# Windowed attention stage: the probabilities' copy is split over ScalarE and VectorE, the inverse is widened on VectorE, and transposes go ahead of scores

## The chip, the cores and the metric

The kernel runs as one program on one core of a Trainium2 chip. It uses the core's engines side by side: TensorE (PE for its matmuls, PEld for its weight loads), VectorE (DVE), ScalarE (ACT), GpSimd (POOL) and SyncE (SP), which here only issues DMAs. Each engine works through its own list of instructions in order; engines wait for one another by semaphores. The metric is the device time of one execution in microseconds.

## The reference

The program is one deep block (windowed attention beside a bidirectional mLSTM, an expert feed-forward) followed by two more layers. The change touches only the windowed attention, which is this part of the reference (8 query heads of 64 columns, 1024 tokens, 256 context tokens, blocks of 128 queries that see the 128 keys before and after them):

```python
def latent_attention(q, k, v, k_ctx, v_ctx, sink):
    ...
    def one_block(args):
        qb, kb, vb, n = args
        ...
        s_loc = jnp.einsum('bqkgd,bskd->bkgqs', qb, kb, preferred_element_type=f32) * scale
        s_loc = jnp.where(ok, s_loc, NEG)
        s_ctx = jnp.einsum('bqkgd,bckd->bkgqc', qb, k_ctx, preferred_element_type=f32) * scale
        s_sink = jnp.broadcast_to(sink_f[None, :, :, None, None], s_loc.shape[:-1] + (1,))
        p = jax.nn.softmax(jnp.concatenate([s_loc, s_ctx, s_sink], -1), -1)
        p_loc = p[..., :span].astype(vb.dtype)
        p_ctx = p[..., span:span + L].astype(vb.dtype)
        return (jnp.einsum('bkgqs,bskd->bqkgd', p_loc, vb)
                + jnp.einsum('bkgqc,bckd->bqkgd', p_ctx, v_ctx))

    o = lax.map(one_block, (q_blk, k_blk, v_blk, jnp.arange(nb)))
```

## The kernel before

The attention stage is `phase_attention`. Its work is cut into 64 units `u`: a unit is one head and one block of 128 queries. Units 2i and 2i+1 are a pair `i` (two heads `a` = 0 and 1, the same block `n`), and there are 32 pairs, 8 blocks for each of 4 values of `j`. A unit has the keys of the context (2 tiles of 128) and of its neighbourhood (3 tiles; 2 in the first and last block). So of 16 units 12 have five tiles and 4 have four; the text calls them long and short.

The order of the work is written out by hand, one list for each engine, with a loop over `u`:

- TensorE: `score(u+2)` makes the scores of two units ahead (4 matmuls into `ps[:, a]`, from `q_st` and the high and low parts of the keys). `turn(u)` transposes the probabilities `p` tile by tile into the PSUM tensor `pt` (called `win_t` in the trace), of which there is one. `weigh(i, ...)` multiplies the turned probabilities by the values, in two pieces: tiles 0 to 2 at even `u`, the rest at odd `u`, for the pair `u // 2 - 1`. Ahead of the first piece it also transposes the pair's inverse denominators, widened to 128 columns, into the second half of `po` (`win_o`).
- VectorE: `largest(u+2)` adds the mask (`win_s`, line 1207; in block 0 the sink too, line 1198) and takes the negative row maximum (line 1209). At odd `u`, `invert(u // 2)` comes before it: the reciprocal of a pair's two denominators (2 columns, line 1216). At even `u`, `take_out(u // 2 - 2)` comes after it: it copies the transposed inverse out of PSUM into `spread` (line 1223) and multiplies the output by it (line 1227).
- ScalarE: `exps(u+1)` makes the probabilities and their sum (line 1169), `take(u)` copies the whole turned unit from `pt` to `p_t` (line 1177, 640 or 512 columns).
- GpSimd: `widen(i)` spreads the two inverses over 128 columns (line 1063). Between two widenings it also does `split_q(j)`, the split of the next two heads' queries into a high and a low part (lines 1076 and 1082), and `pre.split`, the split of two weight tiles for the next stage (lines 336 and 339). It does `split_q(1)` ahead of all widenings, `pre.split` after pair 2, and `split_q(2)` and `split_q(3)` after pairs 8 and 16.

The waits that matter below: `score(u)` waits for `exps(u-2)`, since both use the same half of `ps`; `turn(u)` waits for `exps(u)` and for the copy of unit u-1 out of `pt`; the first piece of `weigh(i)` waits for `widen(i)`.

Of the kernel before, what the change touches and what calls it, by code (L numbers as in the profile page):

```python
# [16 lines left out]
ALU = mybir.AluOpType  # L17
# [3 lines left out]
P = 128  # L21
# [10 lines left out]
N_HEADS, HEAD_DIM = 8, 64  # L32
# [151 lines left out]
def build_program(nc, A, out):  # L184
    with ExitStack() as ctx:
# [786 lines left out]
        def phase_attention():  # L972
# [19 lines left out]
            den = mem("att_den", [P, 2, 2])  # L992
            inverse = mem("att_inverse", [P, 2, 2])
            wide = mem("att_inverse_wide", [P, 2, P])
            spread = mem("att_spread", [P, P])
            zeros = mem("att_zeros", [P, P])
# [11 lines left out]
            probs = sem("win_probs")  # L1008
            p_turned = sem("win_p_turned")
            p_t_out = sem("win_p_t_out")  # L1010
            widened = sem("win_widened")
            inverse_done = sem("win_inverse_done")
# [15 lines left out]
            with nc.psum_tensor("win_s", [P, 2, 2, HALF], F32) as ps, nc.psum_tensor("win_t", [P, 2, HALF], F32) as pt, \  # L1028
# [28 lines left out]
                @block.gpsimd  # L1057
                def _(pool):
                    def widen(i):
                        pool.wait_ge(inverse_done, i + 1)  # L1060
                        if i >= 2:
                            pool.wait_ge(weighed, i - 1)
# [3 lines left out]
                    def split_q(j):  # L1066
                        if j >= 2:
                            pool.wait_ge(scores, 2 * BLOCKS * (j - 1))
                            pool.wait_ge(stacked[j], 32)
                            pool.wait_ge(pre.lo_done, 2)  # L1070
                        for a in range(2):
                            if a:
                                pool.wait_ge(hi_done, 2 * (j - 1) + a)
                            elif j >= 2:
                                pool.wait_ge(widened, BLOCKS * (j - 1) + 1)
# [8 lines left out]
                    pool.memset(zeros[:], 0.0).then_inc(zeroed, 1)  # L1084
                    pool.wait_ge(zeroed, 1)
                    pool.wait_ge(stacked[0], 32)
                    pool.wait_ge(stacked[1], 32)
                    split_q(1)
                    pool.wait_ge(lo_done, 2)
                    for i in range(PAIRS):  # L1090
                        widen(i)
                        if i == 2:
                            pool.wait_ge(widened, i + 1)
                            pre.split(pool)
                        if i % BLOCKS == 0 and BLOCKS <= i < PAIRS - BLOCKS:
                            split_q(i // BLOCKS + 1)
                            pool.wait_ge(lo_done, 2 * (i // BLOCKS + 1))

                @block.tensor
                def _(pe):  # L1100
# [18 lines left out]
                    def turn(u):  # L1119
                        j, n, a = unit(u)  # L1120
                        pe.wait_ge(probs, u + 1)
                        if u:
                            pe.wait_ge(p_t_out, u)
                        for t in range(len(tiles(n))):
                            ins = pe.transpose(pt[:, t // 4, t % 4 * P:(t % 4 + 1) * P], p[u % NP][:, 1 + t * P:1 + (t + 1) * P], ident)
                        ins.then_inc(p_turned, 1)

                    def weigh(i, begin, end):
                        n = i % BLOCKS
                        values = tiles(n)  # L1130
                        if begin == 0:
                            pe.wait_ge(widened, i + 1)
                            if i >= 2:
                                pe.wait_ge(o_out, i - 1)
                            pe.transpose(po[:, i % 2, P:2 * P], wide[:, i % 2, :], ident)
                            pe.wait_ge(p_t_out, 2 * i + 2)
                        for t in range(begin, min(end, len(values))):
# [18 lines left out]
                def _(act):  # L1156
# [4 lines left out]
                    def exps(u):  # L1161
# [3 lines left out]
                        if u >= NP:  # L1165
                            act.wait_ge(p_turned, u - NP + 1)
                        if u >= 4:
# [3 lines left out]

                    def take(u):
                        nt = len(tiles(unit(u)[1]))
                        act.wait_ge(p_turned, u + 1)
                        if u >= NT:
                            act.wait_ge(weighed, u // 2 - 1)
                        act.copy(p_t[:, u % NT, 0:nt, :], pt[:].rearrange("p b (t q) -> p (b t) q", q=P)[:, 0:nt, :]).then_inc(p_t_out, 1)

                    exps(0)
                    for u in range(U):  # L1180
                        if u + 1 < U:
                            exps(u + 1)
                        take(u)

                @block.vector
                def _(dve):
# [6 lines left out]
                    def largest(u):  # L1193
# [11 lines left out]
                        else:  # L1205
# [4 lines left out]
                                          ALU.max, negate=True).then_inc(max_done, 1)  # L1210

                    def invert(i):
                        dve.wait_ge(probs, 2 * i + 2)
                        if i >= 2:
                            dve.wait_ge(widened, i - 1)
                        dve.reciprocal(inverse[:, i % 2, :], den[:, i % 2, :]).then_inc(inverse_done, 1)

                    def take_out(i):
                        j, n = i // BLOCKS, i % BLOCKS
                        dve.wait_ge(weighed, i + 1)  # L1220
                        if i:
                            dve.wait_ge(o_out, i)
                        dve.tensor_copy(spread[:], po[:, i % 2, P:2 * P]).then_inc(spread_out, 1)
# [3 lines left out]
                        dve.tensor_tensor(out_now[:, j % 2, n * P:(n + 1) * P], po[:, i % 2, 0:P], spread[:], ALU.mult).then_inc(o_out, 1)  # L1227
# [2110 lines left out]
```

## Time and profile before

| | us |
|---|---|
| median of 3 runs | 3813.88 |
| lowest and highest run | 3810.36, 3817.38 |
| the profiled execution's own time | 3813.88 |
| its span | 3811.9 |
| attention stage: first score matmul to the last output product | 214.8 to 369.2 |
| loop of the units: first transpose (219.3) to the last product | 149.9 |

The profile gives every group of instructions a line: the source line, the engine, the operation, the tensors written and read, how many there were, the busy time and the mean duration, and then how long the engine had been idle just before them and who ended that idle time. A timeline row gives the start in us, the duration in us and the number of instructions merged. Starts are counted from the beginning of the span. The end of a matmul is modelled, so for TensorE the distances between starts say more than durations do.

### The profile page before, as it was taken

The page shows a single profiled execution, that of the slowest core. Times are in us where ns is not written, and L with a number is a line of the kernel's source. Part 1 is how long each engine was busy: PE and PEld are TensorE (multiplying, and loading weights), DVE is VectorE, ACT ScalarE, POOL GpSimd, SP SyncE. Part 2 cuts the span into 40 slices and gives each one's busy share as a digit, 9 for nine tenths or more (in the row PEclk, how much of TensorE's full clock was granted, in tenths as well). Part 3 has the DMA queues.
Part 4 walks back from the last instruction along what each step waited for, and adds up shares of the span by engine and source line. Part 5 has one row for each costly group of instructions (what it writes and reads, how often), then busy time and mean ns, then how long its engine had stood idle before and what let it go on. Part 6 is the DMA issues. An engine that isn't in the chain of part 4 may idle for free. (4 is left out here: it accounts for less than half of the span.)

```text
span 3811.9 us, 45383 instructions
## 1 busy us (share of the span) xinstructions
PE 3474.8 (91%) x16720; PEld 2808.0 (74%) x16720; DVE 1414.2 (37%) x1976; ACT 1100.2 (29%) x1654; POOL 1380.6 (36%) x678
## 2 busy tenths in 40 slices
PE   8978997779588868999999899999999999999988
PEld 3757885656466646777787688888888888888877
DVE  5566223653666655331111333221222222222232
ACT  4145223431455522100110211111323232232332
POOL 2331331432455545333333444443332333333222
PEclk9979997889799878999999899999999999999999
DMA  8221111043688862132112211132211221121122
GB/s 296 47 78 34 39 28 59 0 137 130 231 300 293 296 178 84 50 110 65 44 39 93 72 50 50 50 110 72 40 39 39 39 45 39 39 39 39 39 56 83
DMA packets 417567, 340.21 MB, mean 89 GB/s; under 512 B 83526, under 2 KB 355706, under 8 KB 417346
## 3 DMA queue, kind: packets, MB, share of 16 engines
q1 hardware_dynamic: 333916, 296.54, 24.7%
q10 hardware_dynamic: 78950, 25.62, 3.1%
q0 software_dynamic: 4608, 16.78, 1.9%
q8 instruction: 62, 1.02, 0.1%
q14 instruction: 31, 0.25, 0.0%
HBM read 287.06 MB, written 48.43 MB: 88 GB/s over the span
## 5 line engine op out<-in xcount | busy, mean ns | idle before, releaser
L273 POOL TENSOR_TENSOR w_hi<-w_raw,zero_col 128x1024 fp32r<-128x1024 f32 x193 | 366.1, 1897 | 1589.4 <-PE first_z L308 640.3
L276 POOL TENSOR_TENSOR w_lo<-w_raw,w_hi 128x1024 fp32r<-128x1024 f32 x193 | 499.5, 2588 | 15.2
L308 PE MATMUL first_z<-h_hi,w_hi 128*128 128x512 f32 x1216 | 392.7, 404 | 4.4 <-DVE h_lo L2059 4.4
L308 PE MATMUL first_z<-h_lo,w_hi 128*128 128x512 f32 x1216 | 377.2, 391 | 0.0
L308 PE MATMUL first_z<-h_hi,w_lo 128*128 128x512 f32 x1216 | 375.6, 390 | 0.0
L308 PEld LDWEIGHTS first_z<-h_hi,w_lo 128*128 128x128 f32 x1216 | 228.8, 188 | 49.7
L308 PEld LDWEIGHTS first_z<-h_lo,w_hi 128*128 128x128 f32 x1216 | 228.9, 188 | 48.8
L308 PEld LDWEIGHTS first_z<-h_hi,w_hi 128*128 128x128 f32 x1216 | 220.3, 189 | 43.4 <-DVE h_lo L2059 4.6
L308 PE MATMUL dil_z<-h_hi,w_hi 128*128 128x512 f32 x640 | 219.0, 423 | 0.6 <-POOLq L264 0.6
L308 PE MATMUL dil_z<-h_lo,w_hi 128*128 128x512 f32 x640 | 199.6, 393 | 0.0
L3251 DVE SCALAR_TENSOR_TENSOR dil_biased<-const,dil_slope_now,dil_aux 128x128 f32<-128x128 f32 (+1 forms) x192 | 78.5, 409 | 322.7 <-PE dil_aux L3103 312.1
L308 PE MATMUL dil_z<-h_hi,w_lo 128*128 128x512 f32 x640 | 197.4, 390 | 0.0
L2387 POOL TENSOR_TENSOR lo_down<-raw_down,hi_down 128x4096 fp32r<-128x4096 f32 x15 | 135.0, 9000 | 149.2 <-ACT hi_down L2475 149.2
L2516 DVE TENSOR_TENSOR lo_gate<-raw_gate,hi_gate 128x2048 fp32r<-128x2048 f32 x30 | 127.1, 4238 | 92.7 <-ACT hi_gate L2475 92.7
L3193 ACT ACTIVATE dil_p<-dil_biased,dil_neg_max 128x128 f32<-128x128 f32 (+1 forms) x192 | 86.3, 450 | 219.8 <-DVE dil_neg_max L3255 219.7
L3294 DVE COPY dil_p_t<-dil_aux 128x128 f32<-128x128 f32 (+1 forms) x192 | 67.8, 353 | 204.2 <-PE dil_aux L3118 181.9
L308 PEld LDWEIGHTS dil_z<-h_hi,w_lo 128*128 128x128 f32 x640 | 120.1, 188 | 27.8
L308 PEld LDWEIGHTS dil_z<-h_lo,w_hi 128*128 128x128 f32 x640 | 120.0, 188 | 26.0
L308 PEld LDWEIGHTS dil_z<-h_hi,w_hi 128*128 128x128 f32 x640 | 112.7, 189 | 16.2 <-POOLq L264 1.0
L3186 ACT ACTIVATE dil_k<-first_z 128x1024 f32<-128x1024 f32 x24 | 40.3, 1680 | 215.4 <-PE first_z L308 121.8
L308 PE MATMUL mls_z<-h_hi,w_hi 128*128 128x512 f32 (+1 forms) x344 | 94.4, 373 | 6.3 <-DVEq L1363 5.9
L336 POOL TENSOR_TENSOR w_hi<-w_raw,zero_col 128x1024 fp32r<-128x1024 f32 x22 | 42.6, 1935 | 153.4 <-DMA w_raw<-in_w_in 62.8
(563 smaller groups left out, 7218.4 us busy)
## 6 DMA issues: line engine op xcount, KB each, us to landing
w_raw<-in_odd_w_in SPq DMA_DIRECT2D x112, 512.0 KB, 3.7
raw_gate<-in_w_gate SPq DMA_DIRECT2D x16, 2048.0 KB, 8.3
raw_up<-in_w_up SPq DMA_DIRECT2D x16, 2048.0 KB, 10.0
raw_down<-in_w_down SPq DMA_DIRECT2D x16, 2048.0 KB, 7.5
w_raw<-in_even_w_in SPq DMA_DIRECT2D x40, 512.0 KB, 3.8
start_w_mod<-in_w_mod SPq DMA_DIRECT2D x16, 1024.0 KB, 7.9
w_raw<-in_w_in SPq DMA_DIRECT2D x16, 512.0 KB, 3.7
w_raw<-in_even_w_out SPq DMA_DIRECT2D x16, 512.0 KB, 3.9
```

The lines of the kernel that those rows point to most:

```text
L273: pool.tensor_tensor(w_hi[:, u], w_raw[:, u], zero_col[:, 0:1].to_broadcast([P, KT * P]).rearrange("p (k n) -> p k n", k=KT), ALU.add).the ...
L276: pool.tensor_tensor(w_lo[:, u], w_raw[:, u], w_hi[:, u].bitcast(F32), ALU.subtract).then_inc(self.split, 1)
L308: ins = pe.matmul(z, w[:, u, kt], rhs[:, kt, c0:c0 + width], start=first, stop=last)
L336: pool.tensor_tensor(w_hi[:, u], w_raw[:, u], zero_col[:, 0:1].to_broadcast([P, KT * P]).rearrange("p (k n) -> p k n", k=KT), ALU.add).the ...
L2387: pool.tensor_tensor(w_lo_["down", slot][:], raw["down", slot][:], w_hi_["down"][:].bitcast(F32), ALU.subtract).then_inc(split["down"], 1)
L2516: dve.tensor_tensor(w_lo_["gate", slot][:, kts], raw["gate", slot][:, kts], w_hi_["gate"][:, kts].bitcast(F32), ALU.subtract).then_inc(spl ...
L3186: act.activation(to, in_banks(z[t % 2][:], t // 2 if t < VT else t - VT), ACT.Copy, scale=P ** -0.5 if t < VT and t % 2 else 1.0).then_inc ...
L3193: act.activation(probs[u][:], biased[:, u % 2, 0:w], ACT.Exp, bias=neg_max[:, u:u + 1], accum_out=den[:, u:u + 1]).then_inc(exp_done, 1)
L3251: dve.scalar_tensor_tensor(out=biased[:, u % 2, 0:w], in0=dist, scalar=slope_now[:, g, :], in1=aux[:, uses % 2, 0:w], op0=ALU.mult, op1=AL ...
L3294: dve.tensor_copy(p_t[:, u % 2, 0:w], aux[:, uses % 2, 0:w]).then_inc(aux_free[uses % 2], 1)
```

## The change

It edits four of the engines' lists in `phase_attention` and nothing else.

- VectorE's reciprocal now reads each of the two denominators 64 times over (a broadcast view) and writes 128 columns; `wide` and `widen` are gone, and with them GpSimd's part in every pair. GpSimd does its three `split_q` and `pre.split` in a plain loop.
- `turn(u)` puts tiles 0 to 2 into the first bank of `pt` and the rest into the second (before: four and one), and signals twice. The copy out of `pt` is split: ScalarE's `take_near` takes 384 columns, VectorE's new `take_far` takes 256 (128 in a short unit). `turn(u)` waits for both copies of unit u-1.
- TensorE does `turn(u)` ahead of `score(u+2)`, where it did it behind.
- VectorE does `take_far(u)` behind `largest(u+2)`.
- The copy of the transposed inverse to `spread` moves from VectorE to ScalarE (`take_spread`, at odd `u`), and `spread` gets two buffers.

```diff
@@ block.gpsimd
-                    def widen(i):
-                        pool.wait_ge(inverse_done, i + 1)
-                        ...
-                        pool.tensor_tensor(wide[:, i % 2, :].rearrange("p (a d) -> p a d", a=2), inverse[:, i % 2, :].unsqueeze(2).to_broadcast([P, 2, HEAD_DIM]),
-                                           zero_col[:, 0:1].unsqueeze(2).to_broadcast([P, 2, HEAD_DIM]), ALU.add).then_inc(widened, 1)
@@ block.tensor
                         pe.wait_ge(probs, u + 1)
                         if u:
-                            pe.wait_ge(p_t_out, u)
+                            pe.wait_ge(near_out, u)
+                            pe.wait_ge(far_out, u)
                         for t in range(len(tiles(n))):
-                            ins = pe.transpose(pt[:, t // 4, t % 4 * P:(t % 4 + 1) * P], p[u % NP][:, 1 + t * P:1 + (t + 1) * P], ident)
-                        ins.then_inc(p_turned, 1)
+                            to = pt[:, 0, t * P:(t + 1) * P] if t < 3 else pt[:, 1, (t - 3) * P:(t - 2) * P]
+                            ins = pe.transpose(to, p[u % NP][:, 1 + t * P:1 + (t + 1) * P], ident)
+                            if t == 2:
+                                ins.then_inc(near_turned, 1)
+                        ins.then_inc(far_turned, 1)
 ...
                         if begin == 0:
-                            pe.wait_ge(widened, i + 1)
+                            pe.wait_ge(inverse_done, i + 1)
 ...
                     for u in range(U):
+                        turn(u)
                         if u + 2 < U:
                             score(u + 2)
-                        turn(u)
                         if u >= 2:
                             weigh(u // 2 - 1, *((0, 3) if u % 2 == 0 else (3, 5)))
@@ block.scalar
-                        act.copy(p_t[:, u % NT, 0:nt, :], pt[:].rearrange("p b (t q) -> p (b t) q", q=P)[:, 0:nt, :]).then_inc(p_t_out, 1)
+                        act.copy(p_t[:, u % NT, 0:3, :], pt[:, 0, 0:3 * P].rearrange("p (t q) -> p t q", q=P)).then_inc(near_out, 1)
+
+                    def take_spread(i):
+                        act.wait_ge(weighed, i + 1)
+                        if i >= 2:
+                            act.wait_ge(o_out, i - 1)
+                        act.copy(spread[:, i % 2, :], po[:, i % 2, P:2 * P]).then_inc(spread_out, 1)
@@ block.vector
+                    def take_far(u):
+                        j, n, a = unit(u)
+                        nt = len(tiles(n)) - 3
+                        dve.wait_ge(far_turned, u + 1)
+                        if u >= NT:
+                            dve.wait_ge(weighed, u // 2 - 1)
+                        dve.tensor_copy(p_t[:, u % NT, 3:3 + nt, :], pt[:, 1, 0:nt * P].rearrange("p (t q) -> p t q", q=P)).then_inc(far_out, 1)
+
 ...
-                        dve.reciprocal(inverse[:, i % 2, :], den[:, i % 2, :]).then_inc(inverse_done, 1)
+                        dve.reciprocal(inverse[:, i % 2, :].rearrange("p (a d) -> p a d", a=2), den[:, i % 2, :].unsqueeze(2).to_broadcast([P, 2, HEAD_DIM])).then_inc(inverse_done, 1)
 ...
                         if u + 2 < U:
                             largest(u + 2)
+                        take_far(u)
                         if u >= 4 and u % 2 == 0:
                             take_out(u // 2 - 2)
```

TensorE's list, before, in the middle of the loop, from one unit's transposes to the next unit's. `win_s` are score matmuls, `win_t` transposes of probabilities, `win_o` the inverse's transpose and the weighing.

```order
L1125 MATMUL win_t<-const,att_p_1473 128x128 x5
L1135 MATMUL win_o<-const,att_inverse_wide 128x128
L1139 MATMUL win_o<-att_p_t,v_rows 64x128 x6
L1115 MATMUL win_s<-k_hi,q_st 128x256
L1116 MATMUL win_s<-k_hi,q_st 128x384
L1115 MATMUL win_s<-k_lo,q_st 128x256
L1116 MATMUL win_s<-k_lo,q_st 128x384
L1125 MATMUL win_t<-const,att_p_1474 128x128 x5
L1139 MATMUL win_o<-att_p_t,v_rows 64x128 x4
```

The same place after the change, from the transposes of one unit to those of the next.

```order
L1112 MATMUL win_t<-const,att_p_1474 128x128 x5
L1100 MATMUL win_s<-k_hi,q_st 128x256
L1101 MATMUL win_s<-k_hi,q_st 128x384
L1100 MATMUL win_s<-k_lo,q_st 128x256
L1101 MATMUL win_s<-k_lo,q_st 128x384
L1130 MATMUL win_o<-att_p_t,v_rows 64x128 x4
L1112 MATMUL win_t<-const,att_p_1472 128x128 x5
```

The transposes stood behind the scores of the unit two ahead and now stand in front of them; the weighing is last in both.

VectorE's list, before, over one pair: mask and maximum at an even unit, the output, then the inverse, mask and maximum at the odd unit.

```order
L1207 TENSOR_TENSOR win_s<-win_s,const 128x2x128
L1209 TENSOR_REDUCE att_neg_max<-win_s 128x1
L1223 COPY att_spread<-win_o 128x128
L1227 TENSOR_TENSOR att_out_now<-win_o,att_spread 128x128
L1216 RECIPROCAL att_inverse<-att_den 128x2
L1207 TENSOR_TENSOR win_s<-win_s,const 128x2x128
L1209 TENSOR_REDUCE att_neg_max<-win_s 128x1
```

The same pair on VectorE after the change.

```order
L1206 TENSOR_TENSOR win_s<-win_s,const 128x2x128
L1208 TENSOR_REDUCE att_neg_max<-win_s 128x1
L1217 COPY att_p_t<-win_t 128x256
L1230 TENSOR_TENSOR att_out_now<-win_o,att_spread 128x128
L1223 RECIPROCAL att_inverse<-att_den 128x128
L1206 TENSOR_TENSOR win_s<-win_s,const 128x2x128
L1208 TENSOR_REDUCE att_neg_max<-win_s 128x1
L1217 COPY att_p_t<-win_t 128x256
```

In each unit a copy of `win_t` has come behind the maximum of the unit two ahead; the copy to `att_spread` is gone, and the reciprocal writes 128 columns instead of 2.

## Rows read from the trace of the kernel before

**Rows 1.** The page's head: span and instructions.
```profile
span 3811.9 us, 45383 instructions
```

**Rows 2.** Window of one pair: PE, PEld, DVE, ACT, POOL busy; granted clock; DMA.
```profile
284.70:288.90 4.20, 4.20 (x42) 3.44 (x39) 3.11 (x8) 3.18 (x7) 0.40 (x1) 1.00 0.00 0
```

**Rows 3.** Waits in 216 to 369 us: total us, times, longest.
```profile
DVE win_s L1207 <- PE win_s L1116: 48.5, 56, 6.1
...
PE win_o L1135 <- POOL att_inverse_wide L1063: 13.2, 4, 3.7
```

**Rows 4.** Timeline of that pair: start, us, engine, line, operation.
```profile
284.74 0.39 PE L1115 MATMUL win_s<-k_hi,q_st 128*128 128x256 f32 x1
...
285.63 0.43 DVE L1207 TENSOR_TENSOR win_s<-win_s,const 128x256 f32<-128x256 f32 x1 [0.36 <-PE win_s L1116]
...
286.10 0.82 DVE L1209 TENSOR_REDUCE att_neg_max<-win_s 128x1 f32<-128x641 f32 x1
...
287.36 0.71 PE L1125 MATMUL win_t<-const,att_p 128*128 128x128 f32 x5
...
287.90 0.27 PE L1135 MATMUL win_o<-const,att_inverse_wide 128*128 128x128 f32 x1
...
288.91 0.39 PE L1115 MATMUL win_s<-k_hi,q_st 128*128 128x256 f32 x1
```

**Rows 5.** Timeline: scores, mask and maximum of a short unit.
```profile
292.96 0.39 PE L1115 MATMUL win_s<-k_hi,q_st 128*128 128x256 f32 x1
...
293.73 0.30 DVE L1207 TENSOR_TENSOR win_s<-win_s,const 128x128 f32<-128x128 f32 x1 [0.51 <-PE win_s L1116]
294.06 0.69 DVE L1209 TENSOR_REDUCE att_neg_max<-win_s 128x1 f32<-128x513 f32 x1
```

**Rows 6.** VectorE groups of the span: PSUM copies, reciprocals (busy us, mean ns | idle).
```profile
L3294 DVE COPY dil_p_t<-dil_aux 128x256 f32<-128x256 f32 x88 | 37.4, 425 | 52.5 <-PE dil_aux L3118 38.7 <-DVE dil_p_t L3294 12.7
...
L3294 DVE COPY dil_p_t<-dil_aux 128x128 f32<-128x128 f32 x104 | 30.4, 292 | 151.7 <-PE dil_aux L3118 143.2 <-DVE dil_p_t L3294 8.3
...
L940 DVE RECIPROCAL qk_rstd<-qk_rstd 128x1024 f32<-128x1024 f32 x4 | 26.2, 6553 | 0.7 <-DVE k_cm L957 0.2
...
L3269 DVE RECIPROCAL dil_den<-dil_den 128x24 f32<-128x24 f32 x8 | 2.4, 296 | 0.0
```

**Rows 7.** Timeline at the loop's start.
```profile
218.10 0.55 PE L1115 MATMUL win_s<-k_hi,q_st 128*128 128x256 f32 x1 [1.23 <-ACT att_p L1169]
...
219.30 1.06 PE L1125 MATMUL win_t<-const,att_p 128*128 128x128 f32 x4
```

**Rows 8.** Timeline at the loop's end.
```profile
363.68 0.69 ACT L1177 COPY att_p_t<-win_t 128x640 f32<-128x640 f32 x1 [0.76 <-PE win_t L1125]
...
364.51 0.63 PE L1125 MATMUL win_t<-const,att_p 128*128 128x128 f32 x4 [0.29 <-ACT att_p_t L1177]
...
368.89 0.29 DVE L1227 TENSOR_TENSOR att_out_now<-win_o,att_spread 128x128 f32<-128x128 f32 x1
```

**Rows 9.** Windows of TensorE behind a stall: busy, granted clock, DMA.
```profile
273.00:276.00 3.00, 3.00 (x17) 0.50 0.69 175
...
279.00:282.00 3.00, 3.00 (x31) 1.00 0.02 5
```

**Rows 10.** Timeline of a long unit at the low clock.
```profile
229.40 0.58 PE L1115 MATMUL win_s<-k_hi,q_st 128*128 128x256 f32 x1
...
230.64 1.27 PE L1125 MATMUL win_t<-const,att_p 128*128 128x128 f32 x5
230.88 0.43 DVE L1207 TENSOR_TENSOR win_s<-win_s,const 128x256 f32<-128x256 f32 x1 [6.13 <-PE win_s L1116]
```

**Rows 11.** Windows of TensorE in the mLSTM stage.
```profile
746.00:750.00 4.00, 3.64 (x30) 1.00 0.00 0
750.00:754.00 4.00, 2.41 (x20) 1.00 0.00 0
...
758.00:762.00 4.00, 1.55 (x8) 0.71 0.00 0
```

More of the change, by code:

```diff
@@ L992, in phase_attention @@
             den = mem("att_den", [P, 2, 2])
-            inverse = mem("att_inverse", [P, 2, 2])
-            wide = mem("att_inverse_wide", [P, 2, P])
-            spread = mem("att_spread", [P, P])
+            inverse = mem("att_inverse", [P, 2, P])
+            spread = mem("att_spread", [P, 2, P])
             zeros = mem("att_zeros", [P, P])
@@ L1008, in phase_attention @@
             probs = sem("win_probs")
-            p_turned = sem("win_p_turned")
-            p_t_out = sem("win_p_t_out")
-            widened = sem("win_widened")
+            near_turned = sem("win_near_turned")
+            far_turned = sem("win_far_turned")
+            near_out = sem("win_near_out")
+            far_out = sem("win_far_out")
             inverse_done = sem("win_inverse_done")
@@ L1058, in _ @@
                 def _(pool):
-                    def widen(i):
-                        pool.wait_ge(inverse_done, i + 1)
-                        if i >= 2:
-                            pool.wait_ge(weighed, i - 1)
-                        pool.tensor_tensor(wide[:, i % 2, :].rearrange("p (a d) -> p a d", a=2), inverse[:, i % 2, :].unsqueeze(2).to_broadcast([P, 2, HEAD_DIM]),
-                                           zero_col[:, 0:1].unsqueeze(2).to_broadcast([P, 2, HEAD_DIM]), ALU.add).then_inc(widened, 1)
-                    def split_q(j):
+                    pool.memset(zeros[:], 0.0).then_inc(zeroed, 1)
+                    pool.wait_ge(zeroed, 1)
+                    pool.wait_ge(stacked[0], 32)
+                    pool.wait_ge(stacked[1], 32)
+                    for j in range(1, N_HEADS // 2):
                         if j >= 2:
@@ L1082, in split_q @@
                             pool.tensor_tensor(q_lo[own[a], :], q_cm[own[a], j, :], q_st[own[a], j % 2, a, :].bitcast(F32), ALU.subtract).then_inc(lo_done, 1)
[L1084 to L1093, printed above, removed]
+                        if j == 1:
+                            pool.wait_ge(lo_done, 2 * j)
                             pre.split(pool)
-                        if i % BLOCKS == 0 and BLOCKS <= i < PAIRS - BLOCKS:
-                            split_q(i // BLOCKS + 1)
-                            pool.wait_ge(lo_done, 2 * (i // BLOCKS + 1))
                 @block.tensor
@@ L1131, in weigh @@
                         if begin == 0:
-                            pe.wait_ge(widened, i + 1)
+                            pe.wait_ge(inverse_done, i + 1)
                             if i >= 2:
                                 pe.wait_ge(o_out, i - 1)
-                            pe.transpose(po[:, i % 2, P:2 * P], wide[:, i % 2, :], ident)
-                            pe.wait_ge(p_t_out, 2 * i + 2)
+                            pe.transpose(po[:, i % 2, P:2 * P], inverse[:, i % 2, :], ident)
+                            pe.wait_ge(near_out, 2 * i + 2)
+                        else:
+                            pe.wait_ge(far_out, 2 * i + 2)
                         for t in range(begin, min(end, len(values))):
@@ L1182, in _ @@
                             exps(u + 1)
-                        take(u)
+                        take_near(u)
+                        if u >= 3 and u % 2:
+                            take_spread(u // 2 - 1)
+                    take_spread(PAIRS - 1)
                 @block.vector
@@ L1214, in invert @@
                         if i >= 2:
-                            dve.wait_ge(widened, i - 1)
-                        dve.reciprocal(inverse[:, i % 2, :], den[:, i % 2, :]).then_inc(inverse_done, 1)
+                            dve.wait_ge(weighed, i - 1)
+                        dve.reciprocal(inverse[:, i % 2, :].rearrange("p (a d) -> p a d", a=2), den[:, i % 2, :].unsqueeze(2).to_broadcast([P, 2, HEAD_DIM])).then_inc(inverse_done, 1)
                     def take_out(i):
                         j, n = i // BLOCKS, i % BLOCKS
[L1220 to L1223, printed above, removed]
                         dve.wait_ge(spread_out, i + 1)
```

11 lines of the change are left out of this document (5 added, 6 removed).

## The prediction

> **What bounds the kernel now.** The span [rows 1] is a chain of stages; the edit lies in one of them, 214.8 to 369.2 us, so I read only that stage. First its windows: over a pair of long units TensorE is busy 4.20 of 4.20 us, VectorE 3.11 and ScalarE 3.18, at the full clock (granted 1.00) [rows 2]. Second the waits: TensorE waits for a widened inverse 4 times, 13.2 us in all, and VectorE waits for scores nearly every unit, 48.5 us in all [rows 3]. Third the timeline: the scores of two neighbouring pairs start 4.17 us apart (284.74 and 288.91) [rows 4]. So the loop goes at TensorE's pace, 2.09 us a unit, and the other two engines wait for it. The exceptions are the four waits: GpSimd's widening stands behind a split of queries or weights on its own queue. Behind such a wait TensorE also runs at the lower of its two levels, 1.2 GHz: granted 0.50 in 273 to 276 us, full again (2.4 GHz) in 279 to 282 [rows 9].
>
> From the first transpose, 219.30, to the transposes of unit 62, 364.51 [rows 7, 8], there are 62 steps in 145.2 us: 2.34 us a unit with the stalls in it, against 2.09 without.
>
> **The change, part by part.**
>
> *Widening on VectorE.* The four waits for GpSimd go, 13.2 us, and the low-clock stretches behind them. If TensorE stayed the bound, the loop would fall to about 62 x 2.09 = 129.6 us (short units are a little quicker): 16 us saved. The price is a reciprocal over 128 columns. From 24 columns in 296 ns and 1024 in 6553 ns [rows 6] one more column costs (6553 - 296) / 1000 = 6.3 ns, so 128 cost 0.296 + 104 x 0.0063 = 0.95 us, once a pair. It is a broadcast read, which the rows do not show; bounds are the 0.30 us of 24 columns and twice the 0.95.
>
> *The copy to `spread`* (about as long as the 128-column copy, 292 ns) goes from VectorE to ScalarE. ScalarE gives up 256 of 640 columns of copy in return, so it stays well under its 3.18 us a pair. It costs nothing while a unit takes over 1.59 us, the half of 3.18.
>
> *The split copy and the order.* This is where it is decided. `turn(u+1)` waits for `take_far(u)`. On VectorE `take_far(u)` stands behind `largest(u+2)`, which waits for `score(u+2)`. On TensorE `score(u+2)` now stands behind `turn(u)`. So there is one closed ring per unit: transposes of u, scores of u+2, mask and maximum of u+2, copy of u, transposes of u+1. Before, `take(u)` on ScalarE needed only `turn(u)` and `exps(u+1)`, not the scores of u+2, and VectorE was not in any one-unit ring; scores of u+2 and VectorE's work on them covered one another's units. Now TensorE can do beside VectorE's part only the weighing. The ring of a long unit:
>
> - transposes to scores: 5 transposes take 287.90 - 287.36 = 0.54 us up to the next matmul [rows 4], 0.56 with the longer weight load of a score;
> - start of the scores to the mask: 285.63 - 284.74 = 0.89 [rows 4];
> - mask to the end of the maximum: 286.10 + 0.82 - 285.63 = 1.29 [rows 4];
> - the copy of 256 columns from PSUM: 0.425 [rows 6], with 0.04 to start: 0.47;
> - its semaphore to the next transpose: ScalarE's copy ended at 364.37 and the waiting transpose started at 364.51 [rows 8]: 0.14. From VectorE it is not shown; bounds 0.04 and 0.24.
>
> Sum 3.35 us. A short unit: 0.45 + (293.73 - 292.96 = 0.77) + (294.06 + 0.69 - 293.73 = 1.02) + 0.33 (292 ns copy) + 0.14 = 2.71 [rows 5, 6]. With 12 long and 4 short in 16: 3.19; with 0.01 for the sink column, 3.20.
>
> *What hides beside the ring.* After the copy of an even unit VectorE also does the output product (about 0.3) and the reciprocal (0.95), 1.3 us with the gaps. It has 0.14 + 0.56 + 0.89 = 1.59 us until the next scores come. So the reciprocal is hidden by 0.3 us; at twice its length it would add 0.65 us a pair, 20 us. The weighing (0.6 to 0.8 us) lies beside mask and maximum (1.29). ScalarE's exponentials of u+1 start when the maximum of u+1 is known and end before the transposes that want them. GpSimd's splits now start as early as their inputs allow and nobody waits for them.
>
> *The clock.* In a long unit TensorE works about 2.0 of 3.35 us and is then idle for 1.3. In the mLSTM stage it was busy 3.64 and 2.41 of 4 us in two windows in a row at a granted 1.00, and fell to 0.71 in one with 1.55 of 4 [rows 11]. The loop, at 60%, is like the 2.41 of 4, so I take the full clock. The start is at the low clock before [rows 10], and three units of it stay there. A low unit costs more: the five transposes 1.27 - 0.71 = 0.56 and the scores up to the mask (230.88 - 229.40 = 1.48) - 0.89 = 0.59 [rows 4, 10], together 1.15. Three times 1.15 is 3.4 us.
>
> *The sum.* `turn(0)` moves from behind the scores of unit 2 to in front: from 219.30 to about 218.24 (these scores started at 218.10, on the same release). Unit 62 is turned at 218.2 + 62 x 3.20 + 3.4 = 420.0 us. The tail stays as it was, 368.89 + 0.29 - 364.51 = 4.7 us [rows 8]: it has no ring, but one wide reciprocal in it and a copy on another engine. End of the stage 424.7 against 369.2: 55.5 us longer. The profiled execution's own time is 3813.88, the same as the median, with a span of 3811.9. So 3813.9 + 55.5 = 3869.
>
> **The rivals.**
>
> *TensorE stays the bound (faster).* If the ring took under 2.34 us a unit (146.3 us over 62 steps is 2.36 with the earlier start), the removed waits would win: 3814 - 16 = 3798. For it speaks that VectorE's sum of work is small, about 4.6 us a pair with the new copies and reciprocal, which over 32 pairs is 147 us, just what the loop takes today. Against it: that is a sum over work that could overlap, and here it stands in one ring with TensorE; mask, maximum and scores alone are 2.18 us, so the transposes and the copy would have to cost 0.2 where rows give about 1.2.
>
> *The clock falls for the whole loop.* Then each long unit takes 4.50 us, and it is 3869 + 59 x 1.15 = 3937. A third of the units low gives 3892. For it: there is idle time in every unit, which the loop of before did not have. Against it: [rows 11], and that at the low clock a unit would keep TensorE busy about 3.9 of 4.5 us, under which the clock came back in [rows 9]. The Trainium skill, page "TensorE: Matmul & The Clock Gate", section "A second HAM failure mode: psum-queue depth-cycling", says that a TensorE that idles briefly between groups of matmuls while it cycles through PSUM banks can swing between its half and full clock. By that rule about half the units would be low, 3903; the mLSTM windows here do not bear it out.
>
> *VectorE's list is the bound inside the slower loop.* If the broadcast reciprocal took twice its width's price, 3869 + 20 = 3889.
>
> *The change does not do what it says.* The four waits could return at another place, since `exps` and `weigh` still wait for `invert`. `invert` of a pair is done at the odd unit, the first piece of its weighing a unit later, so no wait is late; if they did return it would add 13 us, 3882.
>
> **How the numbers follow.** The ring at the full clock: 0.77. The low clock for a third or more of the loop: 0.12. The doubled reciprocal or returned waits: 0.05. TensorE as the bound: 0.04. Something between that loses nothing and wins nothing: 0.02. The predicted time is 3869. Its own range: the semaphore's bounds give 6 us either way, the transposes 4, the copy 4, the start 3 down and 7 up: 3855 to 3886. To leave out no more than 2 in 10 I reach up to the partly low clock: 3854 to 3898. A change of 0.2%, 7.6 us, is about what a measurement of this kernel can tell from none. Faster by more than that 0.04, within it 0.02, slower 0.94.
>
> **What would show it.** The stage should end near 425 us, and neighbouring long units' transposes should start 3.35 us apart at a granted clock near 1.00. The waits should show TensorE's `win_t` waiting for VectorE's `att_p_t` some 60 times, 1.2 to 1.5 us each, and no wait of `win_o` for an inverse; VectorE's wait for scores should be near 0.3 us at odd units and near 1.6 at even ones. The reciprocal should show at 0.95 us and have nobody waiting. The prediction is wrong if `win_t` waits for ScalarE or not at all, or if transposes lie 2.1 us apart.

## The result, and the profile after

The change makes the kernel slower: 3851.41 us (median of 4 runs, 3847.47 to 3854.53) against 3815.63 (4 runs), a ratio of 1.0095 with a 95% interval of 1.0078 to 1.0112. That is 35.8 us more, where 55.5 were forecast; 3851.4 lies 2.6 us under the range's low end of 3854. The direction and the mechanism were right, the size was not. The profiled execution of the changed kernel took 3854.16 us.

From here on the attention stage is measured in one way for all kernels: from the start of the first exponential to the end of the last output product. It was 369.18 - 217.18 = 152.0 us and is 411.25 - 215.70 = 195.6, 43.5 us more. Below are the head of the page after the change, then the rows that mark the stage's first exponential, the transposes of unit 62 and the last output product:

```profile
span 3852.2 us, 45443 instructions
```

```profile
215.70 0.69 ACT L1160 ACTIVATE att_p<-win_s,att_neg_max 128x513 f32<-128x513 f32 x1 [2.49 <-DVE att_neg_max L1208]
```

```profile
406.61 0.63 PE L1112 MATMUL win_t<-const,att_p 128*128 128x128 f32 x4 [0.95 <-DVE att_p_t L1217]
...
410.96 0.29 DVE L1230 TENSOR_TENSOR att_out_now<-win_o,att_spread 128x128 f32<-128x128 f32 x1 [0.99 <-ACT att_spread L1173]
```

The waits of the stage (total us, times, longest), to be set beside [rows 3]:

```profile
PE win_t L1112 <- DVE att_p_t L1217: 61.9, 61, 1.7
DVE win_s L1206 <- PE win_s L1101: 57.4, 56, 2.6
```

There is a new wait, TensorE's transposes for VectorE's copy of `win_t`: 61 times, 61.9 us. The four waits of `win_o` for a widened inverse, 13.2 us, are gone.

The timeline of one long unit at the full clock, to be set beside [rows 4]. It shows the ring in the order of its steps:

```profile
286.79 0.74 PE L1112 MATMUL win_t<-const,att_p 128*128 128x128 f32 x5 [1.22 <-DVE att_p_t L1217]
...
287.29 0.36 PE L1100 MATMUL win_s<-k_hi,q_st 128*128 128x256 f32 x1
...
288.16 0.43 DVE L1206 TENSOR_TENSOR win_s<-win_s,const 128x256 f32<-128x256 f32 x1 [1.51 <-PE win_s L1101]
...
288.62 0.82 DVE L1208 TENSOR_REDUCE att_neg_max<-win_s 128x1 f32<-128x641 f32 x1
289.37 0.41 DVE L1217 COPY att_p_t<-win_t 128x256 f32<-128x256 f32 x1
...
289.70 0.28 DVE L1230 TENSOR_TENSOR att_out_now<-win_o,att_spread 128x128 f32<-128x128 f32 x1
...
289.89 0.94 DVE L1223 RECIPROCAL att_inverse<-att_den 128x128 f32<-128x128 f32 x1
289.93 0.74 PE L1112 MATMUL win_t<-const,att_p 128*128 128x128 f32 x5 [0.89 <-DVE att_p_t L1217]
...
291.29 0.43 DVE L1206 TENSOR_TENSOR win_s<-win_s,const 128x256 f32<-128x256 f32 x1 [0.45 <-PE win_s L1101]
```

The transposes of two neighbouring units start at 286.79 and 289.93, 3.14 us apart, and before every one of them stands a wait for VectorE (0.89 and 1.22 us in turn). The scores start 0.50 us behind the transposes, the mask 0.87 behind the scores. The reciprocal (289.89, 0.94 us) ends at 290.83, and the next mask starts only at 291.29, after a wait of 0.45 us for the scores: it is hidden.

One window of two long units, as [rows 2] was of two (PE, PEld, DVE, ACT, POOL busy; clock; DMA), and one of the loop's middle:

```profile
284.00:290.26 6.26, 4.15 (x41) 3.31 (x40) 4.23 (x9) 2.99 (x9) 0.00 (x0) 1.00 0.00 0
```

```profile
300.00:340.00 40.00, 27.07 (x257) 21.42 (x255) 27.49 (x57) 19.53 (x47) 8.49 (x4) 1.00 0.09 27
```

No engine is full any more: TensorE is busy 27.07 of 40 us, VectorE 27.49 and ScalarE 19.53. This is what a ring looks like in a profile: TensorE and VectorE are each idle a third of the time and each waits for the other.

### The profile page after: what moved, and what is told of

It is laid out like the page before. It is cut to its first block and busy times, and to the rows that moved or that the text cites. A ratio compares the mean times of both kernels' runs of the same rounds, so it can differ in the third digit from the quotient of the medians.

```text
span 3852.2 us, 45443 instructions
## 1 busy us (share of the span) xinstructions
PE 3462.8 (90%) x16720; PEld 2795.9 (73%) x16720; DVE 1445.4 (38%) x2008; ACT 1098.3 (29%) x1686; POOL 1368.9 (36%) x646
## 5 line engine op out<-in xcount | busy, mean ns | idle before, releaser
L273 POOL TENSOR_TENSOR w_hi<-w_raw,zero_col 128x1024 fp32r<-128x1024 f32 x193 | 365.6, 1895 | 1677.0 <-PE first_z L308 640.3
L1112 PE MATMUL win_t<-const,att_p 128*128 128x128 f32 x304 | 47.7, 288 | 63.1 <-DVE att_p_t L1217 61.9
L3190 ACT ACTIVATE dil_k<-first_z 128x1024 f32<-128x1024 f32 x24 | 40.3, 1681 | 218.3 <-PE first_z L308 121.8
```

Source lines behind the costliest of these rows:

```text
L273: pool.tensor_tensor(w_hi[:, u], w_raw[:, u], zero_col[:, 0:1].to_broadcast([P, KT * P]).rearrange("p (k n) -> p k n", k=KT), ALU.add).the ...
L1112: ins = pe.transpose(to, p[u % NP][:, 1 + t * P:1 + (t + 1) * P], ident)
L3190: act.activation(to, in_banks(z[t % 2][:], t // 2 if t < VT else t - VT), ACT.Copy, scale=P ** -0.5 if t < VT and t % 2 else 1.0).then_inc ...
```

## The experiments

All ratios are to the kernel before, run beside them on the same chip. Where a pace is given in us a unit, it is the mean distance between the transposes of unit 44 and those of unit 60, a whole period of 16 units without a stall. It is 2.00 in the kernel before (328.79 to 360.80 us) and 2.98 in the changed one (353.36 to 401.11).

**Cut the ring on VectorE** (`far_first`).

```diff
 (changed kernel, block.vector)
+                        take_far(u)
                         if u + 2 < U:
                             largest(u + 2)
-                        take_far(u)
```

> Theory (a ring per unit through transposes, scores, mask and maximum, and the copy of win_t): with VectorE's copy of win_t ahead of the maximum of the unit two ahead, the copy waits only for the transposes, so the ring is cut. What is left is a ring over two units (exponentials, transposes, scores, mask and maximum: about 3.8 us, 1.9 a unit) and VectorE's own work, 3.8 to 4.6 us a pair. Units 2.1 to 2.3 us apart; TensorE's wait for the copy under 0.2 us; kernel near 3803 us, 45 to 55 below the changed kernel and some 10 below the kernel before. Rival (VectorE has too much work, whatever the order): units stay near 3.1 us apart, kernel near 3850.

Measured: ratio 0.9958 (0.9943 to 0.9972), 3796.8 us, 13.5 under the kernel before and 55 under the changed one, which ran in another session. The stage took 135.5 us (first exponential 216.25, last product 351.75), the pace is 2.05 us a unit, a little quicker than the 2.1 to 2.3 expected, and no wait of TensorE for VectorE's copy is left. The window of the middle of the loop:

```profile
300.00:340.00 40.00, 38.61 (x366) 31.11 (x366) 38.23 (x81) 26.50 (x68) 0.00 (x0) 1.00 0.04 15
```

The same work, in another order, keeps TensorE busy 38.61 of 40 us and VectorE 38.23. So VectorE's work was never too much; its place in the list was. The rival falls.

**Cut the ring on TensorE** (`scores_first`).

```diff
 (changed kernel, block.tensor)
-                        turn(u)
                         if u + 2 < U:
                             score(u + 2)
+                        turn(u)
```

> Theory (the ring): with the scores of u+2 again ahead of the transposes of u, and the copy still behind the maximum, the scores no longer wait for the copy of the unit before, so the ring is cut here too. VectorE waits for scores and then does mask, maximum, copy; units 2.1 to 2.4 us apart, kernel 3800 to 3812. Rival (the split of the copy over two engines is what costs, by its semaphores and VectorE's place in the chain): units stay over 2.8 us apart, kernel over 3835.

Measured: 0.9955 (0.9936 to 0.9973), 3795.2 us, stage 138.1 us (216.20 to 354.25). That is 5 us better than the lower end of what was expected; the pace of 2.11 us a unit is inside it. Here the copy still stands behind the maximum, and nearly all of its cost is gone all the same. It takes both orders together to close the ring; either cut is worth the same within the intervals.

**Take VectorE's copy out of the ring** (`whole_copy`).

```diff
 (changed kernel)
-                            to = pt[:, 0, t * P:(t + 1) * P] if t < 3 else pt[:, 1, (t - 3) * P:(t - 2) * P]
+                            to = pt[:, t // 4, t % 4 * P:(t % 4 + 1) * P]
...
-                        act.copy(p_t[:, u % NT, 0:3, :], ...)
+                        act.copy(p_t[:, u % NT, 0:nt, :], ...)
...
-                        take_far(u)
```

The waits go with the copy: one signal behind the last transpose, one behind ScalarE's copy.

> The turned unit is packed and copied whole by ScalarE again; the wide reciprocal, the move of the spread copy and the transposes ahead of the scores stay. Theory (the ring goes through VectorE's copy alone): no ring per unit, units at TensorE's pace of 2.1 us, no waits for a widened inverse; kernel near 3800, some 15 below the kernel before. Rival (transposes ahead of scores cost by themselves, since scores come 0.5 us later to the maximum and the exponentials): units 2.4 us or more apart, kernel 3820 or more.

Measured: 0.9952 (0.9934 to 0.9970), 3794.5 us, stage 136.6 us, pace 2.09. As the theory said, within the intervals. The split of the copy, which is the change's own idea, brought nothing measurable in this order of TensorE's list: `far_first`, with the ring cut and the copy split, is as fast as this with the copy whole.

**The order on TensorE alone** (`turn_first`): the kernel before, with the two calls swapped as in the change.

> The kernel before with only the two calls on TensorE swapped, transposes of u ahead of scores of u+2. Theory (this order is harmless without VectorE's copy behind the maximum; the ring over two units is 3.8 us, 1.9 a unit, under TensorE's 2.1): within 5 us of the kernel before. Rival (transposes first is itself what costs): 20 us or more slower.

Measured: 1.0011 (1.0001 to 1.0020), 5 us more by the medians (3816.5 against 3811.5), stage 155.2 us against 152.0. Its waits:

```profile
ACT att_p L1169 <- DVE att_neg_max L1209: 48.1, 62, 2.5
...
PE win_t L1125 <- ACT att_p_t L1177: 7.1, 23, 0.9
```

The order is nearly harmless alone, and far from the rival's 20 us. It is not free: the transposes now come 23 times before ScalarE's copy of the unit before has ended, 7.1 us in all, where this happened once, 0.3 us, in the kernel before. The exponentials, which waited for the maximum 8 times (4.5 us) before, now wait 62 times (48.1 us).

**Lengthen the ring** (`ring_plus`). The tensor `neg_max` also gets 32 columns instead of 4, to hold the unused results.

```diff
 (changed kernel, take_far)
+                        dve.tensor_reduce(neg_max[:, 4 + u % 28:5 + u % 28], pt[:, 1, 0:nt * P], AX_X, ALU.max)
                         dve.tensor_copy(p_t[:, u % NT, 3:3 + nt, :], pt[:, 1, 0:nt * P].rearrange("p (t q) -> p t q", q=P)).then_inc(far_out, 1)
```

> The changed kernel with one operation more in the ring: a maximum over the same 256 (or 128) columns of win_t in PSUM on VectorE just ahead of its copy; its result is not used. It takes 0.4 us (0.29 in short units). Theory (everything in the ring costs its whole length each unit): units 0.35 us further apart, 62 x 0.35 = 20 to 25 us more than the changed kernel, near 3875. Rival (the pace is set elsewhere, VectorE waits 57 us for scores anyway): under 5 us more.

Measured: 1.0161 (1.0144 to 1.0178), 3872.1 us against 3850.3 for the changed kernel in the same session, 21.8 more and inside the 20 to 25 expected; stage 214.1 us (216.80 to 430.88), 18.5 more; pace 3.32. The timeline of a long unit with it:

```profile
288.34 0.82 DVE L1208 TENSOR_REDUCE att_neg_max<-win_s 128x1 f32<-128x641 f32 x1
289.08 0.41 DVE L1217 TENSOR_REDUCE att_neg_max<-win_t 128x1 f32<-128x256 f32 x1
...
289.42 0.41 DVE L1218 COPY att_p_t<-win_t 128x256 f32<-128x256 f32 x1
...
289.98 0.97 PE L1112 MATMUL win_t<-const,att_p 128*128 128x128 f32 x5 [0.45 <-DVE att_p_t L1218]
```

The added operation lasts 0.41 us, but from its start to the copy's start there are 0.34 (289.08 to 289.42), and units moved from 3.13 to 3.47 us apart (the last row's transposes are longer because the clock had dipped for a moment there; the 3.47 are from its neighbours). The ring pays for every operation in it, and it pays the distance between starts, not the duration. That distance is the clue to the forecast's error below.

**Shorten what hides beside the ring** (`after_small`).

```diff
 (changed kernel, invert)
-                        dve.reciprocal(inverse[:, i % 2, :].rearrange("p (a d) -> p a d", a=2), den[:, i % 2, :].unsqueeze(2).to_broadcast([P, 2, HEAD_DIM])).then_inc(inverse_done, 1)
+                        dve.reciprocal(small[:, i % 2, :], den[:, i % 2, :]).then_inc(small_done, 1)
+                        dve.wait_ge(small_done, i + 1)
+                        dve.tensor_copy(inverse[:, i % 2, :].rearrange("p (a d) -> p a d", a=2), small[:, i % 2, :].unsqueeze(2).to_broadcast([P, 2, HEAD_DIM])).then_inc(inverse_done, 1)
```

> The changed kernel with a cheaper widening on VectorE: the reciprocal of 2 columns (0.155 us), then a broadcast copy to 128 columns (0.2 us), in place of the 0.94 us reciprocal. Theory (the reciprocal lies hidden in VectorE's wait for scores, 0.45 us of which are left at odd units): no change, within 3 us of the changed kernel. Rival (the reciprocal delays mask and maximum): up to 0.6 us a pair, 15 to 19 us faster.

Measured: 1.0115 (1.0098 to 1.0132), 3854.7 us; the changed kernel in the same session had 1.0101 (1.0084 to 1.0118), 3850.3. No gain: the 4.4 us more lie beyond the 3 that were expected, but the intervals overlap. The stage took 197.9 us (216.97 to 414.83), 2.3 more, at the same pace of 2.99 a unit. Most of that comes from two places, and both lie at a broadcast copy. Here is one, with GpSimd's split of the queries beside it (two operations in one row):

```profile
266.41 4.86 POOL L1081 TENSOR_TENSOR q_lo<-q_cm,q_st 64x1024 fp32r<-64x1024 f32 x2
...
266.66 2.19 DVE L1227 COPY att_inverse<-att_small 128x128 f32<-128x128 f32 x1
...
270.19 0.63 PE L1114 MATMUL win_t<-const,att_p 128*128 128x128 f32 x4 [2.00 <-DVE att_p_t L1219]
```

The broadcast copy, 0.23 us in the median, lasts 2.19 us here and again at 315.55, where GpSimd has just begun the same split (315.29). Each time TensorE's transposes come 3.68 us after the last ones instead of 2.57; behind the second the clock also falls for a moment. The wide reciprocal of the changed kernel took 940 to 946 ns in all 32 cases, beside GpSimd or not.

What the cheaper widening set free turned into waiting, as the mask of an odd unit shows:

```profile
285.34 0.16 DVE L1225 RECIPROCAL att_small<-att_den 128x2 f32<-128x2 f32 x1
...
285.53 0.23 DVE L1227 COPY att_inverse<-att_small 128x128 f32<-128x128 f32 x1
...
286.73 0.43 DVE L1208 TENSOR_TENSOR win_s<-win_s,const 128x256 f32<-128x256 f32 x1 [0.98 <-PE win_s L1103]
```

It waits 0.98 us for the scores where it waited 0.45, and units stay 3.13 us apart.

**The changed kernel again** (`after_again`).

> The changed kernel once more, beside the kernel before on one chip. The two first traces differ by 43.5 us in the attention stage (first exponential to last product) and by 40.3 us in span, the medians by 35.8. Theory (the rest is scatter between runs outside the stage): stage again 195 to 196 us, and more runs bring the difference of the medians to 38 to 44 us. Rival (something outside the stage got quicker with the change): difference again 34 to 37 us, with a stage that is 43 us longer.

Measured: 1.0101 (1.0084 to 1.0118), 3850.3 us against 3811.5, 38.8 us more; stage 195.6 us (216.60 to 412.18). The stage repeats to 0.1 us. The difference of the medians falls between the two bounds that were named: just inside the theory's 38 to 44, and with an interval (32 to 45 us) that holds the rival's 34 to 37 too. This does not settle it.

**The useful part alone** (`wide_only`, and once more as `wide_again`): the kernel before, whose GpSimd list and `invert` are those of the change.

```diff
 (kernel before)
-                            pe.wait_ge(widened, i + 1)
+                            pe.wait_ge(inverse_done, i + 1)
...
-                        dve.reciprocal(inverse[:, i % 2, :], den[:, i % 2, :]).then_inc(inverse_done, 1)
+                        dve.reciprocal(inverse[:, i % 2, :].rearrange("p (a d) -> p a d", a=2), den[:, i % 2, :].unsqueeze(2).to_broadcast([P, 2, HEAD_DIM])).then_inc(inverse_done, 1)
```

> The kernel before with only the reciprocal widened on VectorE and GpSimd's widening gone. Theory (TensorE is the bound, the reciprocal's 0.94 us fits in VectorE's idle time): the four waits, 13.2 us, and the low clock behind them go, 13 to 18 us saved, kernel 3798 to 3802. VectorE's work is 4.0 to 4.1 us a pair against TensorE's 4.17. Rival (VectorE then is too full, the reciprocal in front of the maximum delays the exponentials): units over 2.2 us apart, less than 5 us saved.

> The kernel before with only the wide reciprocal on VectorE, once more, beside its neighbours. Stage 130 to 131.5 us from first exponential to last product, kernel 24 to 28 us under the kernel before.

Measured: 0.9926 (0.9909 to 0.9944), 3784.3 us, and 0.9935 (0.9922 to 0.9949), 3786.6 us. This beats both kernels, by 26 and 27 us against the one before. The stage took 130.8 and 131.0 us, 21 less than 152.0. The window of the loop's middle, of `wide_again`:

```profile
300.00:340.00 40.00, 40.00 (x378) 33.05 (x378) 36.30 (x72) 29.40 (x61) 0.00 (x0) 1.00 0.04 15
```

TensorE is busy 40.00 of 40 us. The saving is more than the 16 us that the forecast had given to the waits, and more than the 13 to 18 expected here. The pace is 2.00 us a unit (in `wide_again` 307.50 to 339.51), as it already was in the kernel before between its stalls; I had taken 2.09 from a single pair of long units and had named the short units as "a little quicker" without counting them. Over 62 units that is 5.6 us, which makes the 21 us of the stage. The 5 or 6 us between these and the medians' 26 and 27 no run explains.

**Three neighbours of it**: the cheap widening (`wide_small`), ScalarE's copy to `spread` (`wide_spread`), and both (`small_spread`), edited as in the experiments above and in the change.

> The kernel before with VectorE widening by a reciprocal of 2 columns and a broadcast copy (0.35 us in place of 0.94 a pair). Theory (the loop is at TensorE's pace already): within 3 us of the wide reciprocal. Rival (VectorE at 4.0 of 4.0 us a pair is the bound there): units 0.05 to 0.15 us closer, 3 to 9 us faster than the wide reciprocal.

> The kernel before with the wide reciprocal and the copy to spread on ScalarE. Theory (ScalarE's copy waits for the weighing in front of the next exponentials, and delays them): equal to or up to 6 us slower than the wide reciprocal alone. Rival (VectorE is the bound and wins 0.28 us a pair): up to 9 us faster.

> The small reciprocal with broadcast copy on VectorE, and the copy to spread on ScalarE. Theory (ScalarE's queue is what the moved copy loads): slower than or equal to the small reciprocal without the move, by 0 to 6 us. Rival: faster than it by 3 us or more.

Measured: 0.9935, 0.9936 and 0.9935, each with the interval 0.9922 to 0.9949 (medians 3790.4, 3788.2 and 3790.7 us, against 3786.6 for `wide_again`); stages of 131.7, 131.4 and 132.8 us. All four are the same within the intervals. With TensorE full, VectorE's 36.30 us of 40 in the wide form against 31.89 in the small one make no difference. The window of `wide_small`:

```profile
300.00:340.00 40.00, 40.00 (x379) 33.00 (x378) 31.89 (x82) 30.27 (x60) 0.00 (x0) 1.00 0.04 15
```

`wide_spread` also shows what the ring's two halves cost once the ring is open. It differs from `whole_copy` in TensorE's order alone, and from `scores_first` in the split of the copy alone. Here is the same window of the three, in the order `wide_spread`, `whole_copy`, `scores_first`:

```profile
300.00:340.00 40.00, 40.00 (x378) 32.92 (x377) 33.83 (x62) 31.22 (x71) 0.00 (x0) 1.00 0.04 15
```

```profile
300.00:340.00 40.00, 38.23 (x361) 30.45 (x361) 32.51 (x60) 29.61 (x69) 0.00 (x0) 1.00 0.04 15
```

```profile
300.00:340.00 40.00, 39.08 (x358) 31.00 (x356) 37.65 (x80) 27.24 (x66) 0.00 (x0) 1.00 0.04 15
```

The paces are 2.00, 2.09 and 2.11 us a unit, the stages 131.4, 136.6 and 138.1 us. So by the traces the order alone costs 5 us and the split alone 7. The ratios (0.9936, 0.9952, 0.9955) go the same way, but their intervals overlap. What was worth having in the change is the widening on VectorE by itself.

## Why the prediction was right and where it was wrong

*The mechanism: right.* A ring of transposes, scores, mask and maximum, and copy; `far_first` and `scores_first` each undid one of its two orders and each gave back the whole loss, `whole_copy` took VectorE's copy out of it with the same result, and `ring_plus` lengthened it and the kernel followed.

*The new wait: right in kind and number, too long in size.* Named as `win_t` for `att_p_t`, some 60 times at 1.2 to 1.5 us; it came 61 times, at 0.89 and 1.22 in turn. The waits of VectorE for the scores, forecast near 0.3 and 1.6 us in turn, were 0.45 and 1.51.

*The reciprocal: right.* 0.95 us was extrapolated from two other widths [rows 6] and 0.942 measured; it was said to hide with 0.3 us to spare and had 0.45, and `after_small` shows that it costs nothing.

*The clock: right in the main.* The granted clock was 1.00 in 300 to 340 us with TensorE busy two thirds of the time, and the first three steps were at the low clock, as forecast. They lasted 3.86, 3.83 and 4.18 us, where the steps at the same place in a later period of 16 units (from units 32, 33 and 34) take 2.89, 2.89 and 3.13. The rival of a low clock for the whole loop did not come true, and neither did the swinging by which the forecast had cited the Trainium skill (page "TensorE: Matmul & The Clock Gate", section "A second HAM failure mode: psum-queue depth-cycling"); that section gives no share of the time, so the half of the units was the forecast's own guess. One of the forecast's reasons was misread: it let the clock come back in [rows 9] at 3.9 of 4.5 us busy, but those rows have TensorE busy 3.00 of 3.00. The loop was not free of the low clock either. There was one short dip in this trace's loop, in these windows of TensorE (busy, clock, DMA), and one step there took 4.18 us instead of 3.13:

```profile
274.00:280.00 6.00, 4.71 (x33) 0.78 0.29 107
280.00:286.00 6.00, 4.16 (x39) 1.00 0.26 69
```

`after_again` dips at the same step; `after_small` has one dip too, at another place, and `ring_plus` two. `far_first`, `scores_first` and `whole_copy`, with the ring cut, have none between 232 us and the end of their loops.

*The failed step: the sum of the ring.* The mechanism held, and the terms of its sum were too long: 3.35 us for a long unit, where 3.14 were measured. Its parts:

| step | forecast us | measured us |
|---|---|---|
| transposes to scores | 0.56 | 0.50 |
| scores to mask | 0.89 | 0.87 |
| mask to the start of the copy | 1.29 + 0.04 | 1.21 |
| copy | 0.43 | 0.41 |
| its end to the next transpose | 0.14 | 0.15 |
| ring | 3.35 | 3.14 |

More than half of the miss is one line. I had let the copy start 0.04 us behind the end of the maximum. It starts 0.07 before that end (288.62 + 0.82 = 289.44, the copy at 289.37). In these rows VectorE has the 0.04 only between operations of which one waits for the other's result, as mask and maximum do (288.16 + 0.43 = 288.59, the maximum at 288.62); the copy, which does not wait for the maximum, starts before it has finished. This was to be read in the trace of the kernel before, in rows I did not use:

```profile
283.86 0.82 DVE L1209 TENSOR_REDUCE att_neg_max<-win_s 128x1 f32<-128x641 f32 x1
...
284.60 0.28 DVE L1223 COPY att_spread<-win_o 128x128 f32<-128x128 f32 x1
```

283.86 + 0.82 is 284.68, and the copy behind it starts at 284.60. The transposes' part was also too long: I had added 0.02 for the longer weight load of a score, and the scores came 0.04 earlier than the next transpose had.

The short unit was too long as well: 2.71 forecast, 316.24 - 313.67 = 2.57 measured, from one unit's transposes to the next's:

```profile
313.67 0.63 PE L1112 MATMUL win_t<-const,att_p 128*128 128x128 f32 x4 [0.55 <-DVE att_p_t L1217]
...
316.24 0.63 PE L1112 MATMUL win_t<-const,att_p 128*128 128x128 f32 x4 [0.88 <-DVE att_p_t L1217]
```

Over the loop: `turn(0)` to `turn(62)` took 406.61 - 216.53 = 190.1 us against 201.8 forecast, 11.7 less. The low clock cost 4.2 us, in the first four steps and the dip, where 3.4 were forecast. That leaves 185.9 us for 62 steps at the full clock, where 62 x 3.20 = 198.4 were forecast: the sum of the ring makes 12.5 us. The start and the end of the loop were as forecast to 0.3 us: the first transposes, at 216.53, start 0.83 us after the first exponential where I had 1.06 (218.24 against 217.18), and the tail was 4.64 against 4.67. So of the 19.7 us by which the forecast was too high, the stage explains 12.

*The remaining 8 us: open.* The stage is 43.5 us longer, the medians only 35.8 and 38.8 apart. The two profiled executions took 3813.88 and 3854.16 us, 40.3 apart, as their spans are; so 4.5 us of the 8 come from where these two executions lie among their kernels' runs. The other 3.2 us lie outside the stage, 1.5 ahead of it (the first exponential at 215.70 against 217.18) and the rest behind it. Outside the stage the traces of this document took between 3649.4 us (`after_small`) and 3662.8 (`small_spread`): 3659.9 in the kernel before, 3656.7 in the changed one, 3653.6 in `after_again`. No edit touches what lies outside the stage. The faster `wide_again` has 3652.5, so a low value does not go with a slow stage. Runs of one kernel scatter by 3 to 17 us here (3792.55 to 3795.37 for `whole_copy`, 3806.18 to 3823.12 for the kernel before in one session), and the interval of either comparison holds 43.5 or comes within 1 us of it. It is most likely scatter, but no run tells it from a small gain outside the stage.

*The range.* It had no term for the scatter of runs. Its own 3855 to 3886 does not follow from the terms named either: they add up to 17 us down and 21 up, which is 3852 to 3890 and still just misses 3851.4.

*The rival on the other side* (TensorE stays the bound, 3798 us) did not happen in the changed kernel. Its price was nearly that of the kernels with the ring cut, 3795 to 3797, but by luck: the pace it assumed was too slow (2.09 against 2.00), and those kernels do not reach 2.00.

## What to carry to other kernels

When engines work through lists, look for rings before adding up work: write down what each operation waits for, including what stands ahead of it in its own list, and see whether a path comes back to its start within one step of the loop. A loop in such a ring costs the sum of its parts, even with both engines in it a third idle, and one swapped pair of calls cuts it. Then try each part of a change alone: here one part was worth 26 us, and the rest took that away and more. For the size of a ring take distances between starts from the trace, at a place where the same kind of operation follows without a wait, not durations with gaps added.

## What the runs showed of the hardware

- In these traces VectorE overlaps neighbouring operations that do not wait for one another: the next starts 0.07 to 0.09 us before the end of the one ahead (289.37 against 289.44, 289.89 against 289.98 and, before the change, 284.60 against 284.68), and an added operation of 0.41 us cost the ring of a long unit 0.34. Where the next waits for the result, it starts 0.03 us after the end (288.59 and 288.62 for mask and maximum; 285.50 and 285.53 for reciprocal and copy in `after_small`).
- VectorE's reciprocal with a broadcast input took 942 ns for 128 columns (mean of 32), and 24 columns without one took 296 [rows 6]: (942 - 296) / 104 = 6.2 ns for each further column, against 6.3 between 24 and 1024 columns. The reciprocal of 2 columns and a broadcast copy to 128 took 0.16 and 0.23 us.
- That broadcast copy, within SBUF, lasted longer at times beside GpSimd: in `after_small` the median is 226 ns and the longest 2190, in `wide_small` 228 and 1389, in `small_spread` 228 and 2322. Each of these copies over 0.3 us ran beside a GpSimd operation on other tensors; no run tests the cause. The reciprocal with the broadcast input stayed at 940 to 953 ns (changed kernel, `wide_only` and `wide_again`), and the changed kernel's 48 copies of 256 columns out of PSUM took at most 416, whatever GpSimd did.
- TensorE was granted the full clock from 300 to 340 us while it was busy 27.07 of 40 us, in pieces of about 2 us with 0.9 to 1.4 us between them. The same loop had one dip to 0.78 in 274 to 280 us, and that step cost 1.05 us more (4.18 against 3.13).
